# Twenty places for expert weights instead of sixteen, seven of them filled during the output projection, in a two-layer trunk on one core

## The reference

```python
def reference(x, ...):                       # x: 256 tokens x 2048, all float32
    for i in range(2):
        h = rmsnorm(x, norm_mix[i])
        x = x + (stick_breaking_mixer if i == 0 else mlstm_mixer)(h, ...)   # in-projection, 16 or 8 heads, out-projection
        h = rmsnorm(x, norm_ffn[i])
        x = x + hierarchical_moe(h, ...)     # top-1 of 4 groups, then top-2 of its 8 experts
    return rmsnorm(x, norm_final)

def hierarchical_moe(h, ...):
    ...                                       # gates: (tokens, 32), two nonzero per token
    hid = silu(einsum('td,edf->tef', t, w1)) * einsum('td,edf->tef', t, w3)     # f = 256
    hid = hid * gates[..., None]
    return einsum('tef,efd->td', hid, w2)
```

## Time and profile before

| | |
|---|---|
| time, median of 3 runs | 1786.22 us (1786.12 to 1786.30) |
| time of the profiled execution | 1786.37 us |
| its span, first to last instruction | 1784.6 us |
| mean granted TensorE clock | 0.946 of full |
| TensorE busy | 1570.1 us, 88% of the span |
| VectorE, ScalarE, GpSimd busy | 731.6, 423.9, 57.7 us |
| moved by the DMA engines | 543.79 MB, 305 GB/s on average |

### The profile page before, as it was taken

The page is one execution under the profiler, slowest core; times in us unless marked ns, Lnnn a source line. Parts: engine busy times, 40 slices in busy tenths (PEclk is TensorE's granted clock), DMA queues, the critical chain, the costliest instruction groups (busy, mean ns, idle before and its releaser), DMA issues.

```text
span 1784.6 us, 25622 instructions
## 1 busy us (share of the span) xinstructions
PE 1570.1 (88%) x9901; PEld 1070.3 (60%) x9901; DVE 731.6 (41%) x1143; ACT 423.9 (24%) x571; POOL 57.7 (3%) x82
## 2 busy tenths in 40 slices
PE   7999999999987788778799999999998877887785
PEld 7999999887433233323287988988863333233331
DVE  4544444444322223222264756657443322222233
ACT  5344343433000000000154334334320000000002
POOL 4010000100000000000011000000000000000000
PEclk9999999999998899889899999999999998899887
DMA  8545455458999999999954465555689999999996
GB/s 270 189 146 181 148 182 166 144 212 313 394 424 425 427 424 425 425 428 424 411 170 141 144 209 168 164 194 175 225 345 426 424 425 425 427 424 425 425 427 268
DMA packets 149419, 543.79 MB, mean 305 GB/s; under 512 B 8736, under 2 KB 25456, under 8 KB 116208
## 3 DMA queue, kind: packets, MB, share of 16 engines
q1 hardware_dynamic: 148448, 541.14, 78.1%
q0 software_dynamic: 912, 1.82, 0.4%
HBM read 540.83 MB, written 2.10 MB: 304 GB/s over the span
## 4 chain that ended last, share of the span: by engine, by line
PE 58%; DMA 29%; SPq 6%; DVE 2%; ACT 2%; issue 1%; DVEq 0%; ACTq 0%
PE psum_G L663 32%; DMA ring<-in_moe_w 29%; PE psum_S L663 16%; SPq L508 6%; PE psum_A L663 6%; PE psum_T L663 3%; DVE w_lo L407 1%; ACT w_hi L403 1%; ACT h L1313 0%; DMA x<-in_x 0%; PE psum_A L670 0%; ACT squares L1147 0%; DVE x L1658 0%; DVE h L1904 0%; PE psum_T L899 0%
## 5 line engine op out<-in xcount | busy, mean ns | idle before, releaser
L663 PE MATMUL psum_A<-ring,arena 128*32 128x512 f32 x1984 | 298.5, 731 | 155.6 <-DMA ring<-in_moe_w 153.9
L407 DVE TENSOR_TENSOR w_lo<-ring,w_hi 128x2048 fp32r<-128x2048 f32 x126 | 289.2, 2298 | 289.2 <-ACT w_hi L403 285.0
L403 ACT CAST w_hi<-ring 128x2048 fp32r<-128x2048 f32 x128 | 244.2, 1908 | 244.6 <-PE psum_G L663 155.8
L663 PEld LDWEIGHTS psum_A<-ring,arena 128*32 128x32 f32 x1984 | 68.1, 122 | 331.9 <-issue 331.6
L1787 DVE COPY arena_two<-psum_A 128x512 f32<-128x512 f32 x64 | 44.3, 692 | 365.8 <-PE psum_A L663 365.4
L1817 DVE TENSOR_TENSOR x<-x,psum_S 128x512 f32<-128x512 f32 x128 | 88.0, 687 | 173.8 <-PE psum_S L663 173.8
L663 PE MATMUL psum_G<-xT_hi,w_hi 128*128 128x256 f32 x512 | 148.8, 291 | 1.1 <-DVE w_lo L407 1.1
L663 PE MATMUL psum_G<-xT_hi,w_lo 128*128 128x256 f32 x512 | 144.7, 283 | 0.0
L663 PE MATMUL psum_G<-xT_lo,w_hi 128*128 128x256 f32 x512 | 144.7, 283 | 0.0
L663 PE MATMUL psum_G<-ring,arena_two 128*32 128x512 f32 x1024 | 121.0, 614 | 22.9 <-DMA ring<-in_moe_w 22.9
L1329 ACT ACTIVATE arena<-psum_T 128x64 f32<-128x64 f32 x64 | 14.3, 224 | 500.0 <-PE psum_T L663 500.0
(11 more groups left out here) (243 smaller groups left out, 2116.3 us busy)
## 6 DMA issues: line engine op xcount, KB each, us to landing
ring<-in_moe_w SPq DMA_DIRECT2D x376, 1024.0 KB, 19.7
ring<-in_sb_w_in SPq DMA_DIRECT2D x48, 1024.0 KB, 5.1
ring<-in_ml_w_in SPq DMA_DIRECT2D x48, 1024.0 KB, 5.1
ring<-in_sb_w_out SPq DMA_DIRECT2D x16, 1024.0 KB, 4.9
ring<-in_ml_w_out SPq DMA_DIRECT2D x16, 1024.0 KB, 5.1
extra_one<-in_moe_w SPq DMA_DIRECT2D x4, 1024.0 KB, 8.6
extra_two<-in_moe_w SPq DMA_DIRECT2D x4, 1024.0 KB, 17.6
x<-in_x SPq DMA_DIRECT2D x2, 1024.0 KB, 6.0
```

The source lines that it names most:

```text
L403: act.copy(w_hi[:, slot_place(j), :], ring[:, slot_place(j), :]).then_inc(hi_made, 1)
L407: dve.tensor_tensor(w_lo[:, slot_place(j), :], ring[:, slot_place(j), :], w_hi[:, slot_place(j), :].bitcast(F32), ALU.subtract).then_inc(l ...
L663: return pe.matmul(dst, lhsT, rhs, start=start, stop=stop, skip_group_check=True)
```

## The change

- **Places.** The expert weights have 20 places: 17 in `ring` (the last reaches into the arena) and 3 where the transposed input lies. In the first quad j = 0 to 19 have a place of their own, 20 and 21 reuse the places of j = 0 and 1, 22 and 23 those of j = 2 and 3. All later quads go round 12 places, those that held j = 4 to 15 of the first quad.
- **Order on SP.** Three expert loads (j = 0, 1, 4) are issued behind pieces 2, 3, 4 of the out-projection with no wait, four (j = 2, 3, 5, 17) behind pieces 10 to 13 after a wait for the end of attention. Then `first_quad`: 6, 7, 16 at the last three `w_lo`; 8 to 13 at the last three reads of `w_hi`/`w_lo`; 14, 15 at the end of the out-projection; 18, 19 at the logits; 20, 21 at the new signal `half_read`; 22, 23 when expert 0 is multiplied. Quad 1 may start its loads when experts 1, 2 and 3 of quad 0 are multiplied.
- **First expert.** TensorE gathers two of the four chunks, multiplies the first half of K, signals `half_read`, and then gathers the other two and multiplies the rest.
- **Space.** `acc` has one buffer instead of two (so `take` also waits until the former one is folded), `y` two chunks instead of four, `disp` one quad instead of all; `slots_of` runs once in each quad. Constants and squares move into the arena. `last_scale` moves into the ring and is loaded at the end of the first quad of layer 1.
- **Between the layers.** `x_final` is signalled before the first `w_lo` of layer 1 is made. The first raw load of layer 1 waits for the last expert's w1/w3 product, no longer for half 0 of the w2 product.

```diff
-SLOTS = 12
+EARLY = {2: 0, 3: 1, 4: 4}
+AT_ATTENDED = {10: 2, 11: 3, 12: 5, 13: 17}
...
+ROUTER_PARTS = ((0, 6), (6, 11), (11, 16))
+LAYER_LOADS = 2 * len(ROUTER_PARTS) + 2
+SMALL_LOADS = LAYER_LOADS + 2 * (KT // 4) + 4
...
+RING = 17
+PLACES = 20
+FIRST_PLACES = [13, 14, 11, 12, 15, 16, 0, 1, 3, 6, 4, 7, 5, 8, 9, 10, 2, 19, 17, 18, 13, 14, 11, 12]
+LATER_PLACES = [15, 16, 0, 1, 3, 6, 4, 7, 5, 8, 9, 10]
...
                     sp_eng.dma_start(ring[:, slot_place(j), :].rearrange("p (k n) -> p k n", k=4),
                                      w[:, 4 * n:4 * n + 4, c * COLS:(c + 1) * COLS]).then_inc(raw_loaded[j % RAW], 16)
+                    if j in EARLY:
+                        moe_load(layer, 0, EARLY[j], True)
+                    if j in AT_ATTENDED:
+                        sp_eng.wait_ge(filled["T1"], first_use["mix", layer]["T1"] + (3 if layer else 2) * NGROUP)
+                        moe_load(layer, 0, AT_ATTENDED[j], True)
...
+            def first_quad(layer):
+                last = len(OUT_ORDER) - RAW
+                for m, j in enumerate((6, 7, 16)):
+                    sp_eng.wait_ge(lo_made, mix_slot(layer, NGROUP, last + m) + 1)
+                    moe_load(layer, 0, j, True)
+                for m in range(HILO):
+                    sp_eng.wait_ge(*split_was_read(layer, NGROUP, last + m))
+                    moe_load(layer, 0, 8 + 2 * m, True)
+                    moe_load(layer, 0, 9 + 2 * m, True)
+                sp_eng.wait_ge(*out_filled(layer, 3, 1))
+                moe_load(layer, 0, 14, True)
+                moe_load(layer, 0, 15, True)
+                sp_eng.wait_ge(filled["T0"], first_use["norm_ffn", layer]["T0"] + 1)
+                moe_load(layer, 0, 18, True)
+                moe_load(layer, 0, 19, True)
+                sp_eng.wait_ge(half_read, layer + 1)
+                moe_load(layer, 0, 20, True)
+                moe_load(layer, 0, 21, True)
+                sp_eng.wait_ge(*up_done(layer, 0, 0))
+                moe_load(layer, 0, 22, True)
+                moe_load(layer, 0, 23, True)
+
+            def later_quad(layer, i):
+                for j in range(6 * QUAD):
+                    if isinstance(i, int) and i == 1 and j in (0, 4, 8):
+                        sp_eng.wait_ge(*up_done(layer, 0, 1 + j // 4))
+                    elif j == 0:
+                        sp_eng.wait_ge(*up_done(layer, i - 1, QUAD - 1))
+                    elif j in (4, 8):
+                        sp_eng.wait_ge(*down_done(layer, i - 1, j // 4 - 1))
+                    elif j in (12, 16, 20):
+                        sp_eng.wait_ge(*up_done(layer, i, j // 4 - 3))
+                    moe_load(layer, i, j, False)
...
-                pool.dma_start(router_w[:, :, 0:GROUPS], moe_w_group[layer]...).then_inc(s, 16)
-                pool.dma_start(router_w[:, :, GROUPS:ROUTER], moe_w_expert[layer]...).then_inc(s, 16)
+                for k0, k1 in ROUTER_PARTS:
+                    pool.dma_start(router_w[:, k0:k1, 0:GROUPS], moe_w_group[layer]...[:, k0:k1]).then_inc(s, 16)
+                    pool.dma_start(router_w[:, k0:k1, GROUPS:ROUTER], moe_w_expert[layer]...[:, k0:k1]).then_inc(s, 16)
...
-            pool.wait_ge(filled["A1"], first_use["moe", 1]["A1"] + 2)
+            pool.wait_ge(filled["G1"], first_use["moe", 1]["G1"] + 5)
             pool.dma_start(last_scale[:, :], norm_final.partition_broadcast(P)).then_inc(last_scale_loaded, 16)
...
+            def first_rows(layer, half):
+                base = first_use["gather", layer]
+                if half == 0:
+                    pe.wait_ge(disp_ready, layer * NQUAD + 1)
+                for c in (2 * half, 2 * half + 1):
+                    pe.wait_ge(h_ready, (4 * layer + c + 1) * TB)
+                    gather(c, base[f"G{c % 2}"] + half)
+                for b in range(2):
+                    pe.wait_ge(emptied[f"G{b}"], base[f"G{b}"] + half + 1)
...
                 for q in range(QUAD):
                     ...
                     for half in up(a, q, first):
+                        if first and q == 0:
+                            first_rows(layer, half)
                         wait_slot(4 * q + 2 * half)
                         wait_slot(4 * q + 2 * half + 1)
...
-                if layer == 0:
-                    split_lo(dve, 1, 0, 0)
-                dve.drain()
...
                 dve.drain().then_inc(x_final, 1)
+                if layer == 0:
+                    split_lo(dve, 1, 0, 0)
...
-    nc = bacc.Bacc("TRN2", target_bir_lowering=False, num_devices=1)
+    nc = bacc.Bacc("TRN2", target_bir_lowering=False, num_devices=1, dynamic_dma_scratch_size=1024)
```

More of the change, by code:

```diff
@@ L275, in build @@
         emptied = {b: sem(f"emptied_{b}") for b in BANKS}
-        slot_loaded = [sem(f"slot_loaded_{n}") for n in range(SLOTS + CSLOT)]
+        slot_loaded = [sem(f"slot_loaded_{n}") for n in range(PLACES)]
+        half_read = sem("half_read")
         raw_loaded = [sem(f"raw_loaded_{n}") for n in range(RAW)]
@@ new lines, in out_stream, with up_done, down_done @@
+                    if j in EARLY:
[3 more added lines that the diff above has]
+                        moe_load(layer, 0, AT_ATTENDED[j], True)
+            def up_done(layer, i, q):
+                a = f"A{q % 2}"
+                return filled[a], i * 2 + (first_use["moe", layer][a] + q // 2 + 1)
+            def down_done(layer, i, half):
+                last = isinstance(i, int) and i == NQUAD - 1
+                return filled["G1"], i * 5 + (first_use["moe", layer]["G1"] + (1 if last else 3) + half + 1)
@@ new lines, in moe_load @@
+            def moe_load(layer, i, j, first):
+                n = place_of(j, first)
+                dst = place_view(n)
+                if j < 4 * QUAD:
+                    w = (moe_w1, moe_w3)[j % 2][layer].rearrange("e (p k) f -> p e (k f)", k=KT)
+                    e, half = j // 4, (j % 4) // 2
+                    src = w[:, bass.ds(i * QUAD + e, 1), half * SLOT:(half + 1) * SLOT]
+                else:
+                    half, e = (j - 4 * QUAD) // QUAD, j % QUAD
+                    w = moe_w2[layer].rearrange("e (k p) n -> p e k n", p=P)
+                    src = w[:, bass.ds(i * QUAD + e, 1), :, half * D // 2:(half + 1) * D // 2]
+                    dst = dst.rearrange("p s (k n) -> p s k n", k=2)
+                sp_eng.dma_start(dst, src).then_inc(slot_loaded[n], 16)
@@ L541, in _ @@
                 out_stream(layer)
[L544 to L554 removed]
+                first_quad(layer)
+                later_quad(layer, 1)
+                with sp_eng.Fori(2, NQUAD) as i:
+                    later_quad(layer, i)
                 if layer == 0:
@@ L977, in route, with gather @@
                 mm(g[:, 0:EXPERTS], ones[:, :], mask[:, 1, :], False, True).then_inc(filled["S0"], 1)
-            def gather(layer, i, c, n):
+            def gather(c, n):
                 bank = f"G{c % 2}"
@@ L996, in up @@
                               w13_tile(q, k, first), k < QUAD, k >= KT - QUAD)
+                    if first and q == 0 and k == 7:
+                        last.then_inc(half_read, 1)
                 last.then_inc(filled[bank], 1)
@@ L1009, in wait_slot @@
                 def wait_slot(j):
[L1010 removed]
+                    pe.wait_ge(slot_loaded[place_of(j, first)], loads_of(layer, i, j, first))
                 def turned(q):
@@ L1023, in turn_gated @@
                         pe.transpose(psum[f"G{b}"][:, 0:P], disp_g[:, b, :], ident[:, :]).then_inc(filled[f"G{b}"], 1)
-                for b in range(2):
-                    pe.wait_ge(emptied[f"G{b}"], i * 5 + base[f"G{b}"])
+                if not first:
+                    for b in range(2):
+                        pe.wait_ge(emptied[f"G{b}"], i * 5 + base[f"G{b}"])
                 for q in range(QUAD):
@@ L1804, in quad @@
                         silu(q - 1)
+                        if q == 1 and more:
+                            slots_of(i + 1)
                     if more:
```

179 lines of the change are left out of this document (73 added, 106 removed).

## The result

The changed kernel takes 1790.12 us (median of 11 runs, 1789.09 to 1793.88), the one before 1786.12 us in the same session (11 runs, 1785.33 to 1786.68). The ratio is 1.0024, 95% interval 1.0016 to 1.0032: slower, by 4.0 us, just beyond the 3.6 us (0.2%) that the forecast took as the least that can be told from nothing. The forecast was 1807 us. The profiled execution took 1790.06 us, its span is 1788.3 us.

What follows compares the result with a forecast made beforehand. Transfers were taken to bound the expert halves, TensorE the mixer halves. From 1786.37 us, gains of 7.7, 10.6 and 2.1 gave 1766.0; a start stall of 40.9 made it 1807 us, range 1763 to 1817.

Steps and rivals of the forecast that it cites:

- The price of a wait: POOL's small loads at the start: each of 13 waits for the large load before costs 4.9 us.
- Part 3: POOL's small loads at the start: smaller descriptor memory makes 13 loads wait, stalling TensorE and adding 40.9 us.
- The forecast's own formula: Whole kernel's time for a wait of s at each of POOL's 13 waiting loads: 1766.0 + 13 s - 22.8.
- The stall: TensorE at the start stands still for 40.9 us, as POOL's last small load lands at 94.2 us.
- Part 1: Expert halves: more places and earlier expert loads end the weight transfers sooner, gaining 7.7 us in layer 0, 10.6 in layer 1.
- The new wait: Expert halves: the 37th load waits for quad 1's first product, leaving layer 0's queue empty from about 485 to 491 us.
- Part 2: Between the layers: signalling x_final before the first w_lo of 2.29 us gains 2.1 us.
- Costed at nothing: Output projection: seven early expert loads behind raw pieces cost 0, with bounds of 0 and 17 us for each layer.
- B: Rival: POOL's small loads do not wait for room in descriptor memory; 1766 us, faster; chance 0.29.
- C: Rival: POOL's waits are short, room free at half the landing time or gate loads in pairs; 1774 and 1787 us; chance 0.13.
- A: The forecast itself: POOL's small loads go one after the other; 1807 us, range 1793 to 1816; chance 0.54.
- D: Rival: early expert loads delay the output projection, up to 17 us for each layer; 1800 us at most, slower; chance 0.04.

Runs made afterwards that it cites:

- experiment 3: Kernel before the change with router loads in three parts and 2048 bytes of descriptor memory for POOL's transfers; 1795.06 us, ratio 1.0048.
- experiment 8: Experiment 4's kernel with expert-weight places reordered so the 37th load no longer waits for quad 1's first product; 1760.97 us, ratio 0.9857.
- experiments 6 and 9: None of the seven early expert loads issued during the output projection: on experiment 4's kernel 1769.05 us, on experiment 8's kernel 1761.61 us.
- experiment 1: Kernel before the change with only 1024 bytes of descriptor memory and router loads in three parts; 1811.22 us, ratio 1.0138.
- experiment 4: Changed kernel with layer 0's small loads issued whole by SP between the third and fourth raw loads, not by POOL; 1769.45 us, ratio 0.9905.
- experiment 11: Experiment 8's kernel with SP's small loads of layer 0 woven between raw pieces instead of in one lump; 1759.29 us, ratio 0.9847.

## Why the prediction was wrong in size and right in direction

**The step that failed is "The price of a wait: ... I take 4.9", one price for all 13 waits.** Part 3's mechanism stood: 13 waits were forecast and 13 are in the trace, at the loads named; VectorE and ScalarE stood behind the last one, TensorE behind them. The mean price was 3.68 us. For the six waits up to the first gate load 4.9 was right (4.97 measured); for the seven between gate loads it was almost twice too high (2.58), and those 7 x 2.3 = 16 us are most of the miss of 16.9. I took the price from the earlier trace rows, where the least landing time is 4.8 us. In those rows about ten of POOL's loads are under way and the DMA share is 1.05 (26.65 to 32.59 us). Time from issue to landing in the changed kernel, gate weights, gate biases, router parts:

```profile
DMA to landing us min/median/max: 2.2/2.3/2.4
...
DMA to landing us min/median/max: 1.6/1.6/1.7
...
DMA to landing us min/median/max: 2.6/4.2/6.3
```

Every one of these goes without another large load of POOL's beside it, and still a router part takes anything from 2.6 to 6.3 us. What goes with it is how busy the DMA engines are with the raw pieces. The windows from issue to landing of the first, second and fourth router part and of the first gate load (DMA share is the last number but one), which landed after 6.0, 2.7, 6.3 and 2.3 us:

```profile
23.00:29.02 6.02, 6.02 (x53) 6.02 (x52) 1.84 (x1) 5.54 (x13) 1.02 (x1) 1.00 0.89 279
29.40:32.10 2.70, 2.70 (x25) 2.70 (x24) 2.34 (x2) 0.95 (x3) 0.83 (x1) 1.00 0.40 140
37.60:43.90 6.30, 6.30 (x54) 6.30 (x54) 3.37 (x3) 1.90 (x1) 0.87 (x1) 1.00 0.89 279
52.80:55.10 2.30, 2.30 (x22) 2.30 (x21) 0.00 (x0) 0.00 (x0) 0.75 (x1) 1.00 0.10 7
```

Of the other parts the third and the fifth fit in (4.9 us at a share of 0.69, 3.5 at 0.72), the sixth less well (2.6 at 0.69). And three gate loads together, but at a share of 0.12 to 0.18 (experiment 3, from 51.59 us), land in 2.2 to 2.7 us. So "they now go singly" is not what makes a wait cheap; quiet DMA engines are, as far as traces alone can tell, for no run varies only that. They were quiet because of the waits themselves: VectorE stood behind the small loads from 46 us on, so SP had no `w_lo` to go on by, and no raw piece was under way when the gate loads went. The forecast had both halves of this, the engines that stop and the price, and did not put them together.

A gate load waits 2.6 us, which is the landing of the one before (2.3) and 0.3. That is what supports that POOL waits for a landing and not for something else; no run separates the landing from the end of the descriptors' use. The Trainium skill's 2.0 us of fixed cost ("DMA: Bandwidth & Descriptors", section "Anatomy of one DMA") was set aside for the measured 4.8; the trace of after is near it for gate loads and biases (1.6 to 2.4 us) and above it for router parts (2.6 to 6.3 us).

The forecast's own formula, with the measured mean, gives 1766.0 + 13 x 3.68 - 22.8 = 1791.0 against 1790.1 measured. That it comes so close is partly luck: the formula gives the last load 5.0 us to land, where it took 1.6, and has no term for the clock, 2.3 us.

**The stall.** Forecast 94.2 + 4.6 - 57.9 = 40.9. With the measured last landing the same line gives 74.8 + 4.6 - 57.9 = 21.5, measured 21.7. It lacks the term of the clock, 2.3 us, which came on top of the stall. (The upper bound does not come out of its own line: a last landing at 134 us gives a stall of 134 + 4.6 - 57.9 = 81 us, not 86.)

**Part 1.** Forecast 7.7 and 10.6 us, measured 8.6 and 10.2, within the 1 to 2 us by which stages vary. The new wait was forecast at 488.9 us; without the shift it ended at 511.9 - 24.0 = 487.9, because the gather in front of it ran at full clock (3.81 us for 32 matmuls, where the kernel before had granted clocks of 0.68 and 0.81 in 433 to 440 us). What the text says beside its sum is wrong: it puts what "the new wait keeps" at 17 to 20 us less the gain, about 9 us for each layer, and experiment 8, which removes the wait, gives back 1.9 and 3.4 us in the two expert halves.

**Part 2.** Forecast 2.1. The traces of before and after have 2.75, the run that undoes it 2.3 by medians, but the forecast's reason, 2.29 us of `w_lo` in front of the signal, is worth 1.1 to 1.3 us in both pairs of traces. The number came out by luck, with 1.5 us of clock.

**Costed at nothing.** Rightly so: no run shows a cost of the early loads (experiments 6 and 9). That they also bring nothing was not in the text: it gave twenty places as the source ("Five more loads before the bottleneck"), which no run isolates, but not that the same places can be filled in time without starting early.

**The rivals.** B (no wait) fell by POOL's timeline and by experiment 1. C had room that comes free before the landing, at s = 2.4 and 1774; the trace shows the opposite, room only when everything has landed. The measured mean price lies between C's and A's, just above the 3.3 us from which A decides against the change: that the result is slower at all hung on 0.4 us for each wait, and the right direction is as much luck as merit. D fell: from the first mask to layer 0's first gather, which takes in the output projection, it is 341.4 to 342.2 us in all traces, with early loads and without.

## What to carry to other kernels

Take the price of a wait from loads that land under the conditions in which they will wait: the same kind of load took 4.8 to 6.2 us on busy DMA engines and 2.2 to 2.7 on quiet ones, and a stall can itself be what makes them quiet. When places are added to a pool, find the load that has to wait next and price its wait. Here that wait kept 5 to 7 us, and as long as it stood it also hid part of what another edit was worth (the half product, 1.8 us with it and 4.2 without), so remove the binding wait before you judge the rest. Before you give a difference of 1 or 2 us between two traces a cause, look whether the same stage varies by as much in runs that do not touch it. Memory taken from a quiet corner, here what was left of POOL's descriptor memory, is paid for by whoever waits in order behind that corner.

## What the runs showed of the hardware that was not expected

- **With little descriptor memory POOL stops at its next load, until all that it has issued has landed**, and the profile calls the time "issue". 13 waits at 1024 bytes, four at 2048 (5.1, 3.9, 6.4 and 3.0 us), none at the library's own size. That a full memory is the reason is inferred from this order of sizes; the profile does not name it.
- **Two stalls of TensorE cost more than their length, others did not.** After 21.7 us without work, and also after 3.8 us, the next 5 us stood at a granted clock of 0.50 (1.2 GHz), where it had been 1.00 before the stall: 2.3 us on top in the changed kernel. Between the layers it stayed at 1.00 after 3.15 us of idle time in the changed kernel, and was at 0.64 and 0.51 (892 to 896 us) after 3.26 us in experiment 4.
- **Short runs hold SP's queue, and the time moves with the order.** The experts' router weights (2048 runs) held SP for 8.23 us right behind another load of 2048 runs (experiment 4) and for 0.51 us when issued 12 us later (experiment 11), where the raw piece behind it was held for 3.76 instead and the eight gate loads ahead of it for 12.07 instead of 6.79. On POOL the first of the earlier trace rows, 2048 runs as well, is 1.35 us of issue. The runs do not show what limits SP there.
